# A decoder step with MoBA attention: decode K pages transposed on VectorE in 32x32 blocks

## The reference

```
gate = einsum('bkgqd,bknd->bkgqn', q, kmean); idx = top_k(gate, 3)
s_sel = q . k_sel * scale;  s_own = q . k_own * scale (causal)
p = softmax(concat(s_sel, s_own));  out = p_sel @ v_sel + p_own @ v_own
```

## Time and profile before

| | us |
|---|---|
| median of 3 runs | 319.69 |
| lowest, highest | 314.59, 324.56 |
| span of the profiled execution, its own time | 318.6 |
| TensorE busy | 289.2 (91%) |
| VectorE busy | 186.8 (59%) |
| ScalarE busy | 152.6 (48%) |
| GpSimd busy | 76.1 (24%) |

### The profile page before, as it was taken

How to read it: one execution, slowest core, us unless ns; L and a number is a source line. 1 busy time by engine, 2 the same in 40 slices (tenths; PEclk the granted TensorE clock), 3 DMA queues, 4 the chain that set the end, 5 groups by cost and what they waited for, 6 DMA issues and landing times.

```text
span 318.6 us, 6275 instructions
## 1 busy us (share of the span) xinstructions
PE 289.2 (91%) x2156; PEld 251.8 (79%) x2156; DVE 186.8 (59%) x412; ACT 152.6 (48%) x342; POOL 76.1 (24%) x95
## 2 busy tenths in 40 slices
PE   0799999990999999989999999999999999999993
PEld 0689997970995876878889899888889896766882
DVE  1774335430733213445635798989898989456672
ACT  3953333430385332643347846465565555537711
POOL 4225322550002112020225441343143041000000
PEclk9999999997899999999999999999999999999999
DMA  7967999999947282944843030400300740421043
GB/s 232 317 192 205 286 307 265 246 267 258 287 132 240 65 259 76 263 135 151 228 150 101 19 124 0 134 0 2 134 0 2 247 167 2 133 91 45 0 148 132
DMA packets 40306, 48.13 MB, mean 151 GB/s; under 512 B 3490, under 2 KB 33186, under 8 KB 40274
## 3 DMA queue, kind: packets, MB, share of 16 engines
q1 hardware_dynamic: 36770, 40.77, 43.7%
q0 software_dynamic: 3504, 6.95, 8.6%
HBM read 40.11 MB, written 3.41 MB: 137 GB/s over the span
## 4 chain that ended last, share of the span: by engine, by line
PE 64%; DVE 16%; DMA 6%; issue 6%; ACT 5%; SPq 1%; DVEq 0%; ACTq 0%
PE Z L1277 11%; PE Z L1278 10%; PE Z L1279 10%; PE T L1230 8%; DMA k_ring<-in_cache_k 4%; DVE probs L1128 3%; PE O L1360 3%; DVE pT_lo L1134 3%; ACT probs L868 2%; DMA x_sb<-in_x_prompt 2%; PE Z L1254 2%; PE S L1254 2%; PE Z L1256 2%; PE S L1255 2%; PE S L1256 2%
## 5 line engine op out<-in xcount | busy, mean ns | idle before, releaser
L1277 PE MATMUL Z<-act_hi,w_hi 128*128 128x256 f32 (+1 forms) x384 | 115.5, 301 | 2.0 <-POOL w_lo L646 1.5
L1278 PE MATMUL Z<-act_lo,w_hi 128*128 128x256 f32 (+1 forms) x384 | 111.5, 290 | 0.0
L1279 PE MATMUL Z<-act_hi,w_lo 128*128 128x256 f32 (+1 forms) x384 | 111.0, 289 | 0.0
L1277 PEld LDWEIGHTS Z<-act_hi,w_hi 128*128 128x128 f32 x384 | 73.2, 191 | 7.9 <-issue 5.2
L1278 PEld LDWEIGHTS Z<-act_lo,w_hi 128*128 128x128 f32 x384 | 73.2, 191 | 0.0
L1279 PEld LDWEIGHTS Z<-act_hi,w_lo 128*128 128x128 f32 x384 | 72.9, 190 | 0.0
L646 POOL TENSOR_TENSOR w_lo<-w_raw,w_hi 128x1024 fp32r<-128x1024 f32 x14 | 33.6, 2399 | 63.0 <-ACT w_hi L732 63.0
L732 ACT ACTIVATE w_hi<-w_raw 128x1024 fp32r<-128x1024 f32 x32 | 33.6, 1053 | 14.4 <-DMA w_raw<-in_w_out 10.9
L868 ACT ACTIVATE probs<-S,nmax 128x128 f32<-128x128 f32 (+3 forms) x32 | 16.6, 524 | 30.7 <-DVE nmax L1118 30.7
L942 DVE TENSOR_TENSOR w_lo<-w_raw,w_hi 128x1024 fp32r<-128x1024 f32 x18 | 21.9, 1223 | 15.5 <-ACT w_hi L732 15.5
L1230 PE MATMUL T<-ident,k_ring 128*128 128x128 f32 x128 | 18.2, 284 | 9.0 <-DMA k_ring<-in_cache_k 8.0
(11 more groups left out here) (219 smaller groups left out, 514.2 us busy)
## 6 DMA issues: line engine op xcount, KB each, us to landing
w_raw<-in_w_in SPq DMA_DIRECT2D x11, 1024.0 KB, 6.5
k_ring<-in_cache_k SPq DMA_DIRECT2D x64, 128.0 KB, 4.1
v_ring<-in_cache_v SPq DMA_DIRECT2D x64, 128.0 KB, 2.7
w_raw<-in_w_out SPq DMA_DIRECT2D x8, 512.0 KB, 4.5
x_sb<-in_x_prompt SPq DMA_DIRECT2D x4, 512.0 KB, 7.3
x_res<-in_x_prompt SPq DMA_DIRECT2D x4, 512.0 KB, 6.0
out<-y_sb SPq DMA_DIRECT2D x8, 256.0 KB, 2.1
w_raw<-in_w_in SPq DMA_DIRECT2D x2, 512.0 KB, 9.0
```

Of the source, the lines that this page charges most:

```text
L1277: mm(out, wh[:, k, :], act_hi[:, k, cols], start=(k == 0), stop=False)
L1278: mm(out, wh[:, k, :], act_lo[:, k, cols], start=False, stop=False)
L1279: last = mm(out, wl[:, k, :], act_hi[:, k, cols], start=False, stop=(k == KD - 1))
```

## The change

**K pages.** A K load now puts page j of four pages of one sequence on partitions 32j to 32j+31, with 4 runs of 32 tokens beside each other. `KTR` m becomes one VectorE transpose of 128x1024 in blocks of 32x32, which leaves 32 channels of a page on each group of 32 partitions. TensorE and ScalarE have no part in it. The 16 steps stand behind halves 2 to 25.

**Scores.** q is laid out by 32 copies of 32 rows, 16 behind half 7 and 16 behind half 9, in two tiles that share memory with zu. `DSC` has 8 steps, one per sequence, of 8 matmuls of 256 columns. The rows of S are now (kv head, page of four, token, head of two) and its columns (sequence, half of the past, token of the page).

**Own tokens.** `DOWN` is one step for both groups: a VectorE transpose of k, two copies of q, and 16 matmuls of 32x32.

**Selection.** Block sums and maxima now lie across rows, so `DSM` transposes small statistics, reduces, spreads them and transposes back. `DEX` has 8 exponentials of 128 columns with a bias for each page, and none writes sums.

**Denominators.** V slots and kv_s have two more columns of ones (`VW` = 258), `DPV` multiplies 258 columns, and `DOD` takes the reciprocal of column 256 of O[1].

**Order.** `DSM`, `DEX`, `DPT` of group 0 go from halves 12, 14, 16 to 18, 19, 20, those of group 1 from 20, 21, 23 to 26, 27, 29; `DPV` of group 1 goes to halves 30 to 37, and `DOD` 1 to 38. Prompt units 0 to 7 all use O[0].

```diff
-    for b in range(4):
-        after(1 + b, ("KTR", 0, 0, b))
+    for m, h in enumerate((2, 4, 5, 7, 9, 10, 11, 13, 14, 16, 17, 18, 21, 22, 23, 25)):
+        after(h, ("KTR", m))
+    for u, h in enumerate((9, 9, 11, 14, 20, 20, 23, 26)):
+        after(h, ("DSC", u))
+    after(16, ("KVN", 4), ("KVN", 0))
+    after(17, ("DOWN",))
+    after(18, ("DSM", 0))
+    after(19, ("DEX", 0))
+    after(20, ("DPT", 0))
     for pg in range(8):
-        after(16 + pg * 3 // 4, ("DPV", 0, pg))
+        after(21 + pg * 7 // 8, ("DPV", 0, pg))
+    after(26, ("DSM", 1))
+    after(27, ("DEX", 1))
+    after(28, ("DOD", 0))
+    after(29, ("DOT", 0))
+    after(29, ("DPT", 1))
     for pg in range(8):
-        after(24 + pg * 3 // 4, ("DPV", 1, pg))
+        after(30 + pg, ("DPV", 1, pg))
+    after(38, ("DOD", 1))
+    after(39, ("DOT", 1))
...
-                    sp.dma_start(k_slot(m)[:, j, :], cache_k[0, bass.ds(at, 1)].rearrange("a s h d -> (a s) (h d)"))\
+                    sp.dma_start(k_slot(m)[32 * j:32 * j + 32, :, :], cache_k[0, bass.ds(at, 1)].rearrange("a (q s) h d -> s (a q) (h d)", s=32))\
...
-                    queue.append((6.8, load_v, m))
+                    queue.append((14.8 + m, load_v, m))
...
+                            for r in range(2):
+                                for x in (0, 1) if n == 3 else (2, 3):
+                                    rows = slice(32 * x, 32 * x + 32)
+                                    for g in range(2):
+                                        for e in range(2):
+                                            frm = g * HD + e * 32
+                                            to = qbd[r][rows, :, :, e, 8 * x:8 * x + 8].rearrange("p b k (t g) -> p k b t g", g=2)[:, :, :, :, g]
+                                            src = q_s[frm:frm + 32, :, 16 * r:16 * r + 16].rearrange("p k (b t) -> p k b t", t=DEC_T)
+                                            ins = nc.vector.tensor_copy(to, src)
                             ins.then_inc(qbd_done, 1)
...
                 elif kind == "KTR":
...
+                    nc.vector.transpose(kT[:, m // 2 % 2, m % 2, :, :, :].rearrange("p q a j -> p (q a j)"),
+                                        k_slot(m).rearrange("p q c -> p (q c)")).then_inc(kt_done, 1)
                 elif kind == "DOWN":
...
+                    nc.vector.transpose(k_own[:, :, :].rearrange("p a t -> p (a t)"), kv_s[:, 0:KVW]).then_inc(k_own_done, 1)
...
+                    for r in range(2):
+                        nc.vector.tensor_copy(q_own[:, r, :, :, :, :].rearrange("p c e b q -> p (c e) b q"),
+                                              qbd[r][0:32, :, :, :, 0:8].rearrange("p b c e q -> p (c e) b q")).then_inc(k_own_done, 1)
...
                 elif kind == "DSC":
+                    u = s[1]
+                    r, b = u // 4, u % 4
+                    if u == 0:
+                        pe.wait_ge(qbd_done, 2)
+                    pe.wait_ge(kt_done, 2 * u + 2)
                     if r:
                         pe.wait_ge(d_exp, r)
+                    for e in range(2):
+                        for c in range(KVH):
+                            last = mm(S[32 * c:32 * c + 32, b * 256:(b + 1) * 256], qbd[r][:, b, c, e, :],
+                                      kT[:, u % 2, :, :, 2 * c + e, :].rearrange("p h q j -> p (h q) j"),
+                                      start=(e == 0), stop=(e == 1))
...
+                    for n in range(8):
+                        cs = slice(n * P, (n + 1) * P)
+                        nc.scalar.activation(pd[:, cs], S[:, cs], ACT.Exp, bias=bbias[:, n // 2, n % 2:n % 2 + 1])
...
+                    link(nc.vector.reciprocal(drec[r], O[1][:, KVW:KVW + 1]))
```

More of the change, by code:

```diff
@@ L258, in build @@
         zu = place("zu", [P, 4, TOK], fp32, R_Z)
+        qbd = [place("qbd0", [P, 4, KVH, 2, 32], fp32, R_Z), place("qbd1", [P, 4, KVH, 2, 32], fp32, R_Z + ZB // 2)]
         zvs = place("zvs", [P, 4, TOK], fp32, R_Z + ZB)
@@ L1029, in _ @@
                 elif kind == "KTR":
[L1030 to L1036 removed]
+                    m = s[1]
+                    dve.wait_ge(k_in[m % 4], 64 * (m // 4 + 1))
@@ new lines, in _ @@
+                    nc.vector.tensor_reduce(red[:, 0:2, :], pairs, AX.X, ALU.add).then_inc(dve_chain, 1)
+                    chain[0] += 1
+                    link(nc.vector.tensor_reduce(red[:, 2:4, :], pairs, AX.X, ALU.max))
+                    link(nc.vector.tensor_copy(red_bc[:, :, :].rearrange("p n (x q) -> p n x q", q=8),
+                                               red[:, :, :].unsqueeze(2).broadcast_to([P, 4, 4, 8])))
+                    link(nc.vector.transpose(full[:, :, :].rearrange("p n c -> p (n c)"), red_bc[:, :, :].rearrange("p n c -> p (n c)")))
@@ new lines, in _, with spread @@
+                    sums = full[:, 0:2, 0:8].rearrange("p u (b e) -> p b e u", e=2)
+                    maxs = full[:, 2:4, 8:16].rearrange("p u (b e) -> p b e u", e=2)
+                    gmin, wmax, tmax, omx, mx, sel = (four[:, n, :] for n in range(6))
+                    def spread(v):
+                        return v.unsqueeze(2).unsqueeze(3).broadcast_to([P, 4, 2, 2])
+                    link(nc.vector.tensor_reduce(gmin, sums, AX.XY, ALU.min))
+                    link(nc.vector.tensor_tensor(pick[:, :, :, :], sums, spread(gmin), ALU.is_equal))
@@ new lines, in _ @@
+                    nc.vector.tensor_reduce(tmax, pick[:, :, :, :], AX.XY, ALU.max).then_inc(dve_chain, 1)
+                    chain[0] += 1
+                    link(nc.vector.tensor_tensor(omx, full[:, 2, 16:20], full[:, 3, 16:20], ALU.max))
+                    link(nc.vector.tensor_tensor(mx, omx, tmax, ALU.max))
+                    nc.vector.tensor_scalar(eight[:, 0, :, :], drop[:, :, :, 0], page_pair[:, 0:1], None, ALU.mult).then_inc(dve_chain, 1)
+                    chain[0] += 1
+                    link(nc.vector.tensor_tensor(sel, mx, ind[:, :], ALU.mult))
@@ L1324, in _ @@
                     if r:
                         pe.wait_ge(d_exp, r)
-                    for c in range(2):
-                        for b in range(4):
-                            last = mm(S[32 * b:32 * b + 32, kk * 512:(kk + 1) * 512], qbd[:, c, r, 32 * b:32 * b + 32], kT[:, c, b, :],
-                                      start=(c == 0), stop=(c == 1))
+                    for e in range(2):
+                        for c in range(KVH):
+                            last = mm(S[32 * c:32 * c + 32, b * 256:(b + 1) * 256], qbd[r][:, b, c, e, :],
+                                      kT[:, u % 2, :, :, 2 * c + e, :].rearrange("p h q j -> p (h q) j"),
+                                      start=(e == 0), stop=(e == 1))
@@ L1330, in _ @@
                     last.then_inc(dsc, 1)
                 elif kind == "DOWN":
-                    r = s[1]
-                    pe.wait_ge(z_hi, 12)
-                    if r:
-                        pe.wait_ge(d_bias, r)
-                    for c in range(2):
-                        last = mm(O[0][:, 0:SMP], qbd[:, c, r, :], kv32[:, c, SEQ:TOK], start=(c == 0), stop=(c == 1))
+                    pe.wait_ge(qbd_done, 2)
+                    pe.wait_ge(k_own_done, 3)
+                    for r in range(2):
+                        for e in range(2):
+                            for c in range(KVH):
+                                last = mm(O[0][32 * c:32 * c + 32, r * SMP:(r + 1) * SMP], q_own[:, r, c, e, :, :].rearrange("p b q -> p (b q)"), k_own[:, 2 * c + e, :],
+                                          start=(e == 0), stop=(e == 1))
```

272 lines of the change are left out of this document (128 added, 144 removed).

## The result

The changed kernel takes **331.05 us** (median of 4 runs, 329.74 to 332.05) against 319.52 us before (4 runs, 314.59 to 324.56) on the same chip: ratio 1.043, 95% interval 1.037 to 1.049. It is slower by 4%. The profiled execution after spans 330.3 us with a mean granted clock of 0.946 (it was the longest of its four), before 318.6 us with 0.988.

What follows compares the result with a forecast made beforehand. TensorE, busy 91% of 318.6 us, was taken as the bound. Terms of -25.4 and +23.5 gave -1.9, the check -4.0; -2.9 was taken, so span 315.7 and median 317 us, range 306 to 326.

Steps and rivals of the forecast that it cites:

- Copies into qbd: Scores behind half 9: TensorE stands 5.6 us for VectorE's 32 small block-diagonal q copies; +6.8 with the clock.
- exponentials: First selection, before the second group's scores: TensorE stands 5.0 us for ScalarE's exponentials; +6.4 with bank and clock.
- q_own: Own-key scores behind half 17: TensorE waits for VectorE's transpose and two copies, +2.9 us (bounds 2, 3.5).
- the second selection's waits: Halves 26 to 29, before half 30: VectorE and ScalarE queues make TensorE wait, +6.2 us (bounds 3, 8).
- The K transpose: VectorE's 128x1024 transpose: no row priced it, taken as 1.2 us from a split of the same shape.
- The rival of VectorE as the bound: K transposes well over 1.2 us make VectorE the bound, deciding from 2.3 us each: 330 us, chance 0.08.
- Until half 39 the attention outputs share one PSUM bank: Prompt attention: VectorE frees the bank 3.2 us before the next product; without that cover each of eight units would pay.
- The clock behind the stops: Lower clock after stops: 1.2 us added behind the qbd stop and 0.8 behind the first selection.
- TensorE's 2.5 us idle absorbs part: V products moved to halves 30 to 37: 5.2 us of work, idle absorbs part, credited -2.5 (bounds 0, -5.2).
- that landing stays: Before half 6: q's staging DMA lands as before while TensorE ends half 4 two us earlier, so +0.8 us.
- -9.8 us: TensorE's 8.0 us wait for K pages goes, with its clock loss, as V loads move to halves 14 to 17.
- The check in the prediction: Blocks laid end to end: half 30 some 6.7 us earlier, 5.2 less 2.5 come back, so -4.0 us.

Runs made afterwards that it cites:

- the bank run: Changed kernel with TensorE's next product into the shared bank waiting for the two additions that read it, not the gate multiply: 327.19 us, 1.034.
- the first try at a new order: Changed kernel with step order alone changed: own-key scores, first selection, its exponentials and second group's scores behind later halves: 329.98 us, 1.042.

## Why the prediction was wrong

- **Right:** the stops and their places. Copies into qbd 5.7 us (5.6 predicted), exponentials 4.0 (5.0), q_own 2.4 (2.9), the second selection's waits 6.1 together (6.2). The K transpose is 1.234 us (1.2), the waits for K pages are gone, and by the end of half 16 the kernel leads by 7.2 us. The rival of VectorE as the bound is refuted by the doubled transposes.
- **The failed step:** "Until half 39 the attention outputs share one PSUM bank; cover: VectorE frees it 3.2 us before the next product starts", costed at nothing. The 3.2 us hold for two banks. In the earlier trace rows the multiply that ends at 202.0 is that of unit 3 and the product at 205.18 that of unit 5, the next into the same bank only while units alternate. With one bank the next is unit 4, and its product started 2.4 us before that multiply ended:

```profile
199.57 0.28 PE L1423 MATMUL O<-pT_hi,v_st 128*128 128x256 f32 x1
```

  In that trace each of the units 0 to 7 ends its multiply 0.25 to 3.0 us behind the start of the next unit's product, so there was no cover to count on, and the prediction itself said that without it each unit would pay. In the kernel after three products waited, those of units 2, 6 and 8, 4.8 us together, and halves 39 and 41 took 4.67 and 4.76 us instead of 3.4. By these rows it is the largest term, 7.4 us; the bank run gave 6.5 in the profiled execution (5.7 of them from half 30 on) and 3 to 4 in the times.
- **The clock behind the stops.** Predicted 2.0 us for two of them. Of halves alone, 18, 30, 39 and 41 took 4.60, 4.77, 4.67 and 4.76 us where 3.10 (even) and 3.44 (odd) are usual, 5.7 us together, 2.6 of them behind the bank's waits. The scores behind the stop for qbd and those behind the stop for the exponentials took 3.64 us each where the first try at a new order has such scores in 1.93, and the transposes behind the latter 1.74 where it has 1.09:

```profile
62.08 3.64 PE L1379 MATMUL S<-kT,qbd 128*32 128x256 f32 x32 [5.70 <-DVE qbd L1032]
112.16 3.64 PE L1379 MATMUL S<-kT,qbd 128*32 128x256 f32 x32 [3.99 <-ACT p_own L866]
115.73 1.74 PE L1294 MATMUL T<-ident,pd 128*128 128x128 f32 x8
```

```profile
120.08 1.93 PE L1379 MATMUL S<-kT,qbd 128*32 128x256 f32 x32
121.95 1.09 PE L1294 MATMUL T<-ident,pd 128*128 128x128 f32 x8
```

  That makes 9.8 us, or 7.2 without the bank's part, 5.2 more than predicted: the most mis-sized of the terms that had a price. I had scaled one long stop (1.8 us lost for 8.0); here stops of 1.7 to 5.7 us lost 1.2 to 2.4 each. Not every stop did: half 6 ran in 3.09 us behind a wait of 2.4, and half 18 in 3.13 in the run with half of the copies later, behind the same wait of 2.4 that precedes 4.60 here. No run separated the clock from the stops.
- **"TensorE's 2.5 us idle absorbs part":** net +2.7 was predicted for the moved V products; six pages cost 3.6 us, eight at that price 4.8, so nothing was absorbed.
- **The front:** "that landing stays" gave +0.8; half 6 started 1.9 us later instead of 1.9 earlier (four blocks of 0.68 less the 0.8). GpSimd's selects (7.42 us for 16, not named in the prediction) delay half 0, and GpSimd's load of the spatial weights by 3.2 us: the prediction had named that chain and taken its time as fixed. Without the selects half 6 was still no earlier, since the weights' load then came in among the staging; with that load moved too, half 6 came 1.2 us earlier than in the kernel after and 0.8 later than in the kernel before.

```profile
3.03 7.42 POOL L651 TENSOR_SCALAR_AFFINE_SELECT own_mask<-own_mask 32x32 f32<-32x32 f32 x16
```

- **"-9.8 us" for the K wait** was right as a piece of trace (14.9 us less from half 10 to the end of half 16, blocks included), and yet the old order did not keep it: with the V loads alone moved, 0.4% remained. In the kernel after TensorE waits for no V page; whether that is owed to the new stops in front of them was not run.
- The check in the prediction had half 30 start 6.7 us earlier; it started 1.5 earlier. Of the 5.2 us between, 3.8 stand before half 6. Halves 21 to 30 took 7.2 us more than before, 6.1 of them the waits of the second selection; single V pages at 0.6 in place of pairs at 1.00 and the clock (0.86 from 142 to 164 us) are there in the trace, and no run separated them.
- Halves 39 to 47 took 2.4 us more than before even with the bank mended (50.1 against 47.6). A wait of 1.1 us for the copies of `DOT` 1, which the change put behind half 39 and the prediction did not price, is in it; the rest is open.
- Together these terms are more than the 14.6 us between the predicted and the measured span (-2.9 and +11.7): they overlap, and the stops for the exponentials and for q_own were 1.5 us shorter than priced.

## What to carry to other kernels

Price a stop with what may run behind it at the lower clock: here 1.2 to 2.4 us on top of most stops of 1.7 to 5.7 us. A chain of small dependent steps has a length of its own: count how many steps of the bound engine cover it, and what else its engine must deliver in that time. Where two buffers become one, read the cover between uses that are neighbours in the new order, since a pair that shares a buffer in the old trace is one use further apart. Look for the worst of all uses, and release the buffer at its last read, not at the end of the step.

## What the runs showed of the hardware

- Four fp32 products of 258 columns into four groups of 32 output partitions took 0.64 us, one took 0.62.
- VectorE's transpose in 32x32 blocks of 128x1024 fp32 took 1.234 us, about as long as a subtraction of that shape (1.215).
- 19.7 us more of these transposes cost 4 to 5 us of time.
- K pages written onto 32 partitions landed in 3.5 us median against 3.1 onto 128.
- A VectorE multiply of 128x128 fp32 took 0.29 us alone and 2.15 to 2.40 when a GpSimd subtraction of 128x1024 (2.35 to 2.38) had started 0.1 to 0.4 us before it.
